# Matrix products that nobody reads, placed in TensorE's idle stretches of a two-layer transformer kernel

## The reference

```python
y_lat, y_ctx = token_mixer(modulate(x, sh_a, sc_a), modulate(xc, ...), ...)   # MLA + Fourier + neighbourhood
x   = layer_norm(alpha * x + g_a * y_lat, ln1_g[l], ln1_b[l])
h_f = modulate(x, sh_f, sc_f)
f   = hier_moe(h_f, ...)        # group by softmax top-1, then top-2 of its 8 experts; 32 experts in all
x   = layer_norm(alpha * x + g_f * f, ln2_g[l], ln2_b[l])
```

## Time and profile before

| | |
|---|---|
| median of 3 executions | 2784.84 us (2782.38 to 2792.76) |
| profiled execution | 2782.9 us, of which the span from first to last instruction is 2781.0 us |
| TensorE matmul busy | 2490.5 us, 90% of the span |
| VectorE, ScalarE, GpSimd busy | 921.9, 626.6 and 347.8 us |
| mean granted TensorE clock | 0.954 of full |
| DMA | 604.39 MB, 217 GB/s mean |

### The profile page before, as it was taken

The page is one execution under the profiler, slowest core; times in us unless marked ns, Lnnn a source line. Parts: engine busy times, 40 slices in busy tenths (PEclk is TensorE's granted clock), DMA queues, the critical chain, the costliest instruction groups (busy, mean ns, idle before and its releaser), DMA issues.

```text
span 2781.0 us, 32912 instructions
## 1 busy us (share of the span) xinstructions
PE 2490.5 (90%) x12755; PEld 1550.2 (56%) x12755; DVE 921.9 (33%) x1708; ACT 626.6 (23%) x1172; POOL 347.8 (13%) x409
## 2 busy tenths in 40 slices
PE   5999899999999789989985899899999888989994
PEld 3769556788884443333332659567887433433331
DVE  2345466522223720000004434556332630000003
ACT  2231444622210110111102321446331000111110
POOL 1341000001111221000002330000011210000001
PEclk8999999999999789999998999999999879999997
DMA  9571000322217679999996461003333779999994
GB/s 273 187 260 46 6 1 13 75 69 57 69 42 222 238 297 418 421 420 419 420 421 234 155 220 45 7 1 75 102 91 117 278 320 419 421 420 404 421 421 167
DMA packets 238331, 604.39 MB, mean 217 GB/s; under 512 B 67328, under 2 KB 143504, under 8 KB 188640
## 3 DMA queue, kind: packets, MB, share of 16 engines
q1 hardware_dynamic: 210786, 528.65, 50.5%
q0 software_dynamic: 24512, 63.13, 6.5%
q10 hardware_dynamic: 2880, 10.49, 0.9%
HBM read 585.70 MB, written 38.16 MB: 224 GB/s over the span
## 4 chain that ended last, share of the span: by engine, by line
PE 69%; DMA 13%; DVE 7%; SPq 4%; ACT 4%; issue 2%; POOL 1%; DVEq 0%; ACTq 0%; POOLq 0%
PE slot L1067 19%; PE abank L672 18%; PE vbank L672 10%; DMA arena<-in_w_up_e 6%; PE slot L978 5%; DMA arena<-in_w_down_e 3%; DMA arena<-in_w_gate_e 2%; PE vbank L854 2%; SPq L2556 2%; DVE nmx L1479 1%; PE slot L881 1%; PE abank L752 1%; PE vbank L664 1%; PE vbank L801 1%; ACT arena L1970 1%
## 5 line engine op out<-in xcount | busy, mean ns | idle before, releaser
L1067 PE MATMUL slot<-arena 128*64 128x512 f32 (+2 forms) x3264 | 827.0, 616 | 84.9 <-DMA arena<-in_w_up_e 59.1
L1067 PEld LDWEIGHTS slot<-arena 128*64 128x64 f32 (+2 forms) x3264 | 296.5, 147 | 562.5 <-issue 550.6
L672 PE MATMUL abank<-round,round 128*128 128x512 f32 (+1 forms) x1792 | 492.7, 356 | 12.8 <-DVE round L1544 8.3
L672 PEld LDWEIGHTS abank<-round,round 128*128 128x128 f32 x1792 | 319.9, 190 | 75.8 <-issue 19.1
L1786 DVE TENSOR_TENSOR arena<-slot,arena 128x512 f32<-128x512 f32 x76 | 52.6, 692 | 808.3 <-ACT arena L2090 516.0
L672 PE MATMUL abank<-hT_low,round 128*128 128x512 f32 (+1 forms) x896 | 319.6, 357 | 0.0
L672 PE MATMUL vbank<-round,round 128*128 128x512 f32 (+2 forms) x1312 | 307.5, 361 | 2.0 <-issue 2.0
L672 PEld LDWEIGHTS vbank<-round,round 128*128 128x128 f32 x1312 | 227.4, 190 | 37.0 <-issue 3.2
L672 PEld LDWEIGHTS abank<-hT_low,round 128*128 128x128 f32 x896 | 169.7, 189 | 23.6
L1570 DVE TENSOR_TENSOR arena<-vbank,arena 128x512 f32<-128x512 f32 x72 | 43.4, 603 | 308.1 <-PE vbank L672 308.1
L978 PE MATMUL slot<-arena 128*128 128x512 f32 x320 | 140.1, 599 | 3.4 <-POOL arena L2251 3.4
(11 more groups left out here) (282 smaller groups left out, 2705.8 us busy)
## 6 DMA issues: line engine op xcount, KB each, us to landing
arena<-in_w_gate_e SPq DMA_DIRECT2D x128, 1024.0 KB, 26.9
arena<-in_w_up_e SPq DMA_DIRECT2D x128, 1024.0 KB, 27.1
arena<-in_w_down_e SPq DMA_DIRECT2D x128, 1024.0 KB, 28.0
arena<-in_w_ada POOLq DMA_DIRECT2D x80, 512.0 KB, 4.9
arena<-in_w_in SPq DMA_DIRECT2D x48, 512.0 KB, 4.1
arena<-in_w_in SPq DMA_DIRECT2D x8, 2048.0 KB, 13.3
h_rows<-arena ACTq DMA_DIRECT2D x20, 512.0 KB, 6.7
arena<-y_rows SPq DMA_DIRECT2D x20, 512.0 KB, 7.5
```

What stands on the lines that cost most here:

```text
L672: last = pe.matmul(to, x, y, start=(k == 0 and q == 0), stop=(k == len(terms) - 1 and q == 2))
L1067: last = pe.matmul(to[at, cols], x[:, at], w[:, at_w, :], start=first, stop=final)
```

## The change

A helper `keep_clock(bank, count)` issues `count` products of the 128 x 128 identity with 512 columns of constants into a PSUM bank that is free at that time. Nothing reads the result and nothing is signalled. It is called five times in each layer: 4 products behind router `nq - 3`, 3 behind router `nq - 2`, 6 behind the last router, 4 ahead of the first expert rows, and 9 behind the loop for overflow blocks and ahead of the merge's waits. One wait is added ahead of the first call (the tile before the last must have been taken from its slot).

```diff
@@ -612,6 +612,11 @@
                 last.then_inc(mixed, 1)
+
+            def keep_clock(bank, count):
+
+                for _ in range(count):
+                    pe.matmul(bank[:, 0:512], ident, cst[:, 0:512], start=True, stop=True)
 
             def input_biases(L):
 
@@ -990,8 +995,14 @@
                     if n >= 3:
                         router(n - 3)
-                for n in range(len(qt) - 3, len(qt)):
-                    router(n)
+                spare = slot[len(qt) % 2]
+                router(len(qt) - 3)
+                pe.wait_ge(slot_taken_v, before(L) + len(qt) - 1)
+                keep_clock(spare, 4)
+                router(len(qt) - 2)
+                keep_clock(spare, 3)
+                router(len(qt) - 1)
+                keep_clock(spare, 6)
 
                 pe.wait_ge(route_v, 2 * L + 1)
                 ps = vec()
@@ -1051,6 +1062,7 @@
                     close(pe.matmul(ps[0:1, NX:NX + 1], xe[0:NE, 0:1], ones[0:NE, 0:1], start=True, stop=True), vgroups)
 
+                keep_clock(slot[0], 4)
                 xt_done, at_done = {}, {}
 
@@ -1169,6 +1181,7 @@
                 with pe.Fori(0, NX // 2) as turn:
                     extra_block(turn * 2 + 1, 1, turn)
                     extra_block(turn * 2 + 2, 0, turn + 1)
+                keep_clock(slot[0], 9)
                 pe.wait_ge(share_ready, L + 1)
                 for n in range(4):
                     mix(L, n)
```

## The result

The changed kernel takes 2790.27 us (median of 20 executions, 2782.31 to 2799.04) against 2782.94 us of the kernel before (20 executions, 2779.16 to 2792.76): ratio 1.0023, 95% interval 1.0016 to 1.0030. It is slower by 6 to 7 us, a quarter of a percent (the interval is 4.5 to 8.3 us). The profiled execution (2786.1 us, span 2784.2) is one of the quick ones, 4 us under its median; that of the kernel before (2782.9) lies at its median.

The account below looks back on a forecast made before the run. It took TensorE's clock to be below full in short stretches, with saturated DMA engines bounding the experts; 14.5 us lost at the merge less 5 gained made 9.5 slower, from the median 2784.84 to 2794 us, range 2781 to 2803.

Parts of the forecast that it names:

- Price of a product: Each added product is two records on TensorE: 0.86 us at full clock, 1.72 us at half clock.
- Part 1: Products between the last routers: hidden or late, last router at fuller clock; +1.0 us a layer, bounds +2.4 and -3.8.
- Rival (a): Three products ahead of router 5 run at half clock and delay it: 1.5 us lost a layer, 2802 us; chance 0.17.
- Part 2: Six products during VectorE's choice of experts: counting gains 1.0 us, placing and ranking 0 (bounds 0 and 3.3).
- Part 3: Four products ahead of expert rows: first expert product 1.0 us late, its 64 records 1.5 us shorter; net +0.5 us.
- The first weight load behind the 16: Sign in the weight stream after the router stretch: this load would come earlier by about 2.5 us.
- 5 us in both layers: Total gain ahead of the experts, 2.5 us a layer; bounds some 18 us gained and 14 lost.
- Part 4: Nine products ahead of the merge start late behind the loop and delay `mix(0)`: 14.5 us lost in both layers, bounds 12 and 16.
- nothing in the change moves the loop: Overflow loop's last closing branch stays at 1489.6 us (layer 0), so the nine products start about half a microsecond before `mix(0)`.
- the 3 to nearly 7 us that I allowed: Time the nine merge products would run at half clock before it rises: 3 to 7 us.
- Rival (b): Clock holds from the projections to the experts: about 9 us gained a layer, 2781 us; chance 0.13.
- Rival (c): Merge products start in the idle 12 us and cost nothing: 2.7 us gained a layer there, 2774 us; chance 0.05.

Follow-up runs that it names:

- routers_only: The changed kernel without the nine products ahead of the merge, the other four groups kept: 2778.4 us, 0.9984 to the kernel before.
- guarded_nine: The changed kernel with TensorE's ten-turn loop inside one branch, not taken, the nine products still behind it: 2771.28 us, 0.9963 to the kernel before.
- in_turns: The changed kernel with the nine products taken out and one product at the head of each loop turn: 2776.48 us, 0.9971 to the kernel before.
- rows_two: guarded_fill with 2 instead of 4 products ahead of the first expert rows: 2771.47 us, 0.9961 to the kernel before.
- guarded_fill: The changed kernel with TensorE's loop inside one branch and 14 (layer 0) and 11 (layer 1) merge products instead of nine: 2774.9 us, 0.9970.
- merge_only: The kernel before with only the nine products behind the loop added, in both layers: 2800.14 us, 1.0058 to the kernel before.
- guard_only: The kernel before with TensorE's ten-turn loop inside one branch, not taken, no products added: 2784.34 us, 1.0004.

## Why the prediction was right

The time forecast was 2794 against a median of 2784.84; the difference was +9.5 us, measured +7.3 (ratio 1.0023, where 9.5 us are 1.0034). The terms, in its own order:

- *Price of a product.* Right: 3.45 us for 8 records at full clock (`mix(0)`, 1492.42), 5.4 for 12 in other kernels.
- *Part 1, +1.0 a layer.* In this trace the mechanism was right (hidden in the gap, late router bound by VectorE), the size was not: 2.3 us in both layers, next to the upper bound of 2.4. I had given much weight to a clock that is down when the three products start. It was down (to 946.8) only inside the four before them. Rival (a) did not happen in this trace, but in layer 0 it is the usual case. In seven of the nine kernels that have both groups (all but the changed one and routers_only) the clock fell in or just ahead of router 4's logits, the three products ran at half clock for most of their time, and router 5 started 1.8 to 2.2 us behind its row tile. The one of guarded_nine, layer 0 (router 4's logits, the three products, router 5's transposes), whose row tile was there at 950.4:

```profile
944.79 2.92 PE L969 MATMUL vbank<-arena 128*128 128x36 f32 x16 [0.84 <-ACT arena L2080]
947.51 5.26 PE L619 MATMUL slot<-cst 128*128 128x512 f32 x6
952.61 1.04 PE L963 MATMUL abank<-cst,arena 128*128 128x128 f32 x8
```

  It did not cost what the rival said, because router 5 then ran at full clock: in those seven the last logits were taken 26.5 to 27.9 us behind E, against 26.96 before. (The two latest, in_turns with 27.94 and rows_two with 27.46, had a row tile that was 1.8 and 1.2 us late as well.) Over all nine, layer 0 gained 0.5 us on average and layer 1 gained 1.6: the +1.0 a layer is about what the kernels show, and the 2.3 of the changed kernel's trace is the good end. Over five kernels with the four groups ahead of the experts (the changed one, routers_only, guarded_nine, in_turns, guarded_fill) the 65th expert record starts 72.7 and 67.7 us behind E on average, against 77.3 and 70.3 in three without them (before, merge_only, guard_only): 4.6 and 2.7 us, 7.2 in both. The profiled execution of the changed kernel had 9.6 of it and is quicker than its median.
- *Part 2, +1.0 and 0.* 1.9 and 1.2 in counting; +1.2 and -0.3 behind it.
- *Part 3, +0.5.* -0.9 + 1.5 = 0.6 and -2.1 + 2.5 = 0.4. Right in both layers, and by its two opposite terms. The first weight load behind the 16 came 6.0 us earlier behind E in layer 0 (55.8 against 61.8), where 2.5 were forecast.
- *5 us in both layers* was too little, 9.6 in this trace and 7.2 on average.
- *Part 4, -14.5.* The deciding step, and right in kind: the products stand behind the loop, begin when the clock is down, and push `mix(0)` back; merge_only and guarded_nine show it from both sides. Its size was 12.6 in this trace (3.9 and 8.7), inside the bounds of 12 and 16, but neither layer is near the 7.2 that I gave it; that the two errors cancel is luck. The step "nothing in the change moves the loop" was wrong: in layer 0 the loop ended 2.6 us sooner behind the last expert records, and the products had 2.9 us of head start on the landing instead of 0.5. In layer 1 it ended 1.6 us later, and they started 1.1 after the rows had landed. Both are the long branch: 2.84 us before and 0.35 after in layer 0, 0.35 and 1.83 in layer 1. I had read the loop's end and not what it was made of. The nine ran 3.2 and 5.2 us at half clock before it rose (6.2 and 5.3 in merge_only), so the 3 to nearly 7 us that I allowed hold; no row of the kernel before showed the upper one.
- *Rival (b)*, the clock holds throughout: no, 0.82 in the stretch, it fell three times. *Rival (c)* was not the case as the kernel stands. guarded_nine is nearest to it, and its 2771 lies near the 2774 that I named, but not by the same sum: I had given 2.7 us a layer to the merge and 5 to the routers, and by its trace it was -0.9 and +2.5, 8.2 ahead of the 65th expert record, and the 2 us at the end.

The forecast was right in sign and place, and in the step that decides. Both terms were off in the same direction, too slow: 5 us of gain forecast and 9.6 in the trace, 14.5 of loss forecast and 12.6. That is why the two profiled executions differ by 3.2 us and not by 9.5; between the medians it is 7.3, nearer to the forecast than the terms deserve. Over several kernels the gain ahead of the experts is 7.2 us and not 9.6 (above), which goes that way; the rest of the 4 us between the trace and the median is not accounted for.

## What to carry to other kernels

Work that is to fill an idle stretch can't start before whatever holds the sequencer in that stretch is through: look at the queue's own instructions (loops and branches whose bodies are skipped), not only at the engine's idle time. Here a branch around the empty loop let the nine products start; the plainest other way, the nine ahead of the loop as it stands, was not run. A product without a reader that is through before the next real one is due was free here; one that isn't pushes the real one back, and whether that pays depends on what the clock then gives (about even in front of layer 0's last router, a loss in front of `mix(0)`). Measure such groups one by one: here those of the routers and of the choice gained 1 to 2 us in their own stretch (too little to see in the total), one gave back what it took, one was on the wrong side of a loop, and the kernel with one more, ahead of the placing, had the lowest median.

## What was not expected of the hardware

The clock fell at 943.4 us in the changed kernel, 0.9 us into a run of 512-column products, behind narrow logits: wide work begun just ahead of the fall did not prevent it. And one branch of an empty loop took 1.8 to 2.9 us instead of 0.2, in one layer or both. It goes with the transfers on the instruction queue. That queue of the changed kernel (transfers, MB, share), layer 0 (1471 to 1476 us) and layer 1 (2723 to 2727 us):

```profile
q8 instruction: 1, 0.02, 1.2%
...
q8 instruction: 2, 0.03, 2.7%
```

Layer 0, with one transfer, has no long branch, and layer 1, with two, has one. So it is in all five kernels that walk through the loop: in the six layers with a branch of 1.8 us or more, two transfers of 16 KB begin between the start of the last 16 expert records and 6 us later, and in the four layers without one, a single transfer. The first of the two begins at the same moment as the long branch in layer 0 of the kernel before (1476.3 us), but 0.6 us behind its start in merge_only, layer 0, and 0.5 ahead of it in the changed kernel, layer 1. That the branch waits for the loop's code is argued from this, not shown by an experiment, and with one trace of each kernel it is open whether the kernel or the execution decides which layers have it.
